# Third block, joint stretch: the head norms' root and reciprocal as one power on GpSimd, 128x512 at a time

## The reference, cut to what matters

```
def rms_norm(x, g):
    xf = x.astype(jnp.float32)
    y = xf * lax.rsqrt(jnp.mean(jnp.square(xf), axis=-1, keepdims=True) + RMS_EPS)
    return y * g

def l2_normalize(x):
    xf = x.astype(jnp.float32)
    return xf * lax.rsqrt(jnp.sum(jnp.square(xf), axis=-1, keepdims=True) + RMS_EPS)

# gdn_mixer: after the short convolution and silu
    q = l2_normalize(q.reshape(B, T, GDN_HEADS, GDN_HEAD_DIM))
    k = l2_normalize(k.reshape(B, T, GDN_HEADS, GDN_HEAD_DIM))
# third_block: the attention's output, per head
    o_na = rms_norm(o_na, na_norm_g[l]).reshape(B, T, NA_WIDTH).astype(x.dtype)
```

## Time and profile before

| what | value |
|---|---|
| median of 3 runs | 4870.76 us (4870.22 to 4872.85) |
| profiled execution, its own time | 4873.72 us |
| its span, first to last instruction | 4872.4 us |
| busy over the span: PE, PEld, DVE, ACT, POOL | 85%, 66%, 39%, 28%, 8% |
| mean granted TensorE clock | 0.914 of full speed |

### The profile page before, as it was taken

The page is one execution under the profiler, slowest core; times in us unless marked ns, Lnnn a source line. Parts: engine busy times, 40 slices in busy tenths (PEclk is TensorE's granted clock), DMA queues, the critical chain, the costliest instruction groups (busy, mean ns, idle before and its releaser), DMA issues. The chain is left out here.

```text
span 4872.4 us, 52741 instructions
## 1 busy us (share of the span) xinstructions
PE 4119.7 (85%) x19748; PEld 3208.3 (66%) x19748; DVE 1906.7 (39%) x2890; ACT 1376.7 (28%) x2125; POOL 394.7 (8%) x260
## 2 busy tenths in 40 slices
PE   5876999996998879999995787885687687999997
PEld 2653478774767758888884565554576565888885
DVE  2135232214465443222234255653544455332333
ACT  3224221212465141111112355562221222111111
POOL 0010000000004100000003000002223211000002
PEclk7987999997999989999997798997898888999999
DMA  1101011111112111111110211111101000111111
GB/s 58 39 13 43 0 52 48 43 40 57 42 34 79 35 48 48 48 47 47 52 41 8 75 37 37 45 48 69 36 1 35 18 27 27 48 47 48 51 48 52
DMA packets 77748, 203.59 MB, mean 42 GB/s; under 512 B 18176, under 2 KB 19520, under 8 KB 77448
## 3 DMA queue, kind: packets, MB, share of 16 engines
q1 hardware_dynamic: 77576, 201.35, 12.8%
HBM read 188.14 MB, written 15.14 MB: 42 GB/s over the span
## 5 line engine op out<-in xcount | busy, mean ns | idle before, releaser
L462 PE MATMUL b_ffn_acc<-b2f_x_lo,b_ffn_wh 128*128 128x512 f32 x832 | 327.5, 394 | 0.0
L461 PE MATMUL b_ffn_acc<-b2f_x_hi,b_ffn_wh 128*128 128x512 f32 x832 | 325.5, 391 | 0.7 <-DVE b_ffn_wl L521 0.7
L463 PE MATMUL b_ffn_acc<-b2f_x_hi,b_ffn_wl 128*128 128x512 f32 x832 | 325.4, 391 | 0.0
L477 ACT ACTIVATE b_ffn_wh<-b_ffn_raw 128x1024 fp32r<-128x1024 f32 (+2 forms) x148 | 149.3, 1009 | 615.7 <-PE b_ffn_acc L463 612.1
L521 DVE TENSOR_TENSOR b_ffn_wl<-b_ffn_raw,b_ffn_wh 128x1024 fp32r<-128x1024 f32 (+2 forms) x148 | 184.9, 1250 | 234.0 <-ACT b_ffn_wh L477 202.9
L461 PE MATMUL b_ffn_acc<-b3f_x_hi,b_ffn_wh 128*128 128x512 f32 x512 | 201.3, 393 | 18.0 <-DVE b_ffn_wl L521 18.0
L462 PE MATMUL b_ffn_acc<-b3f_x_lo,b_ffn_wh 128*128 128x512 f32 x512 | 203.2, 397 | 0.0
L463 PE MATMUL b_ffn_acc<-b3f_x_hi,b_ffn_wl 128*128 128x512 f32 x512 | 200.1, 391 | 0.0
L461 PE MATMUL b_ffn_acc<-b3f_hidden_hi,b_ffn_wh 128*128 128x512 f32 x512 | 199.2, 389 | 0.0
L463 PE MATMUL b_ffn_acc<-b3f_hidden_hi,b_ffn_wl 128*128 128x512 f32 x512 | 199.2, 389 | 0.0
L462 PE MATMUL b_ffn_acc<-b3f_hidden_lo,b_ffn_wh 128*128 128x512 f32 x512 | 199.2, 389 | 0.0
(11 more groups left out here) (549 smaller groups left out, 9242.9 us busy)
## 6 DMA issues: line engine op xcount, KB each, us to landing
b_ffn_raw<-w SPq DMA_DIRECT2D x64, 512.0 KB, 3.3
b_ffn_raw<-w_ffn SPq DMA_DIRECT2D x44, 512.0 KB, 3.5
b_out_raw<-w_out SPq DMA_DIRECT2D x16, 512.0 KB, 3.4
b_ffn_raw<-w_ffo SPq DMA_DIRECT2D x16, 512.0 KB, 3.4
g_heads<-na_done SPq DMA_DIRECT2D x16, 512.0 KB, 2.9
na_feed_raw<-w_gqkv SPq DMA_DIRECT2D x24, 256.0 KB, 2.9
all_x<-xT SPq DMA_DIRECT2D x8, 512.0 KB, 6.6
b_v_raw<-w_bv SPq DMA_DIRECT2D x16, 256.0 KB, 2.6
```

Source lines behind the costliest of these rows:

```text
L461: nc.tensor.matmul(acc[i][:, c], wh[i][:, wk], xh[:, c], start=(k == 0), stop=False)
L462: nc.tensor.matmul(acc[i][:, c], wh[i][:, wk], xl[:, c], start=False, stop=False)
L463: last = nc.tensor.matmul(acc[i][:, c], wl[i][:, wk], xh[:, c], start=False, stop=(k == st.KT - 1))
L477: nc.scalar.activation(wh[i][:, 0:st.KT * P], raw[i][:, 0:st.KT * P], ACT.Copy).then_inc(hi_done, 1)
```

## The change

The copy out of the accumulation bank adds 1e-6 on the way (Identity with a bias in place of Copy). The square root on ACT and the two reciprocals on DVE go. GpSimd gets a strand of its own: after its memsets it fills a 128x1 column with -0.5 and raises each half of `na_norm_root` to that power, once the half's copy is there. The scalings on DVE are as before, at the same due times, and wait for `inverted`, which GpSimd now increments.

```diff
@@ HeadNorms.__init__
+        self.power = ph.sb(f"{name}_power", [P, 1])
-        self.copied, self.rooted = ph.sem(f"{name}_copied"), ph.sem(f"{name}_rooted")
+        self.copied = ph.sem(f"{name}_copied")
@@ HeadNorms.roots
-                self.nc.scalar.activation(self.root[:, c], self.bank[:], ACT.Copy).then_inc(self.copied, 1)
-            yield self.starts[m] + 6.0
-            se.wait_ge(self.copied, 2 * m + 2)
-            self.nc.scalar.activation(self.root[:], self.root[:], ACT.Sqrt, bias=1e-6).then_inc(self.rooted, 1)
+                self.nc.scalar.activation(self.root[:, c], self.bank[:], ACT.Identity, bias=1e-6).then_inc(self.copied, 1)
+
+    def powers(self, pool):
+        self.nc.gpsimd.memset(self.power[:], -0.5)
+        pool.drain()
+        for m in range(len(self.jobs)):
+            for half in range(2):
+                c = slice(half * HALF, (half + 1) * HALF)
+                pool.wait_ge(self.copied, 2 * m + half + 1)
+                self.nc.gpsimd.tensor_tensor(self.root[:, c], self.root[:, c], self.power[:].broadcast_to([P, HALF]), ALU.pow).then_inc(self.inverted, 1)
@@ HeadNorms.scaling
-            for half in range(2):
-                c = slice(half * HALF, (half + 1) * HALF)
-                yield self.starts[m] + 7.5 + 0.7 * half
-                if half == 0:
-                    ve.wait_ge(self.rooted, m + 1)
-                self.nc.vector.reciprocal(self.root[:, c], self.root[:, c]).then_inc(self.inverted, 1)
@@ neighbourhood_attention, block.gpsimd
                 pool.drain().then_inc(padded, 1)
+                norms.powers(pool)
```

## The result

The changed kernel takes 6655.49 us (6648.05 to 6656.54) against 4871.81 us before in the same runs: a ratio of 1.3656, 95% interval 1.3632 to 1.3680, 1783.7 us more. The forecast was 5004 us, its range ended at 5290. The sign was right; the size was not, by a factor of 13.

What follows compares the result with a forecast made beforehand. No engine was full; waits between in-order engines, with norm jobs in DVE's queue, set the stretch. Delay 118 plus port 33 less ACT's 18 gave +133 us, so 5004 us; forecast range 4910 to 5150, whole range 4800 to 5290.

Steps and rivals of the forecast that it cites:

- What comes, and its price: On POOL, 24 powers of 128x512, each taken as two reciprocal-like steps of 6.1 us: 12.3 us.
- the upper end: Longest time allowed for one POOL power: four reciprocal-like steps, 24.5 us.
- First copy's end + 2t: Earliest start of DVE's second scaling, after two successive POOL powers of t each: 24.6 us at t = 12.3.
- 24t - 162: Kernel's time change in us, t being one power's duration: +133 at 12.3 us, break-even at 6.75.
- The windows: From a norm job's first copy's end to DVE's second scaling: twelve before the change, sum 176.9 us, mean 14.7.
- +33: Cost in us of DVE's taps, low parts and other window work pushed aside by POOL's powers.
- -18: Credit in us for work ACT sheds, about half of 35.8 us.
- The rival (c): Power far dearer than two hard steps, POOL becoming the stretch's bound: +426 us, 5297 us at t = 24.5; chance 0.12.
- The port: DVE's two-input instructions and POOL's contend for SBUF ports, locked for a whole instruction; 33 us added.
- ACT's relief: ACT sheds roots, their table loads and six loads back, 35.8 us in all; 18 credited.
- The rival (a): Cheap power on POOL, the change pays: -66 us at t = 4, at most 115 us gained; chance 0.24.

Runs made afterwards that it cites:

- the single power: Kernel before, only the first half of the eleventh norm job through GpSimd's power: 4941.9 us, ratio 1.0140; with its scaling planned late, 4864.72 us, ratio 0.9985.
- the plain multiplications above: Kernel before, plus 300 plain 128x512 multiplications on GpSimd scratch tiles from the joint stretch's start, results unused: 4931.48 against 4870.86 us, ratio 1.0125.
- that run: Changed kernel with the power replaced by a multiplication by 0.001 on GpSimd, norms not computed: 4805.17 against 4875.99 us, ratio 0.9855.

## Why the prediction was wrong

**The step that failed** is "What comes, and its price". It took 12.3 us for a power, from two steps each as hard as DVE's reciprocal at POOL's plain rate, and closed the range at four such steps, 24.5 us. It measured 81.9 us, 6.7 times the 12.3 and thirteen of the steps of 6.1. The 6.1 us that the value and the upper end came from was itself built, from DVE's reciprocal and the ratio of two plain instructions, and no row shows how POOL computes a power. "At least" two such steps is also the wording of a floor, not of a ceiling. So the upper end was not a bound, and it carried the 5290. What takes POOL 0.159 us per column inside a power no run shows.

**The mechanism and its multiplier were right.** "First copy's end + 2t" is what the timeline shows (163.9 us), and with t = 81.9 the sum 24t - 162 gives +1804 us; measured is +1784, within 1.2%. The windows alone give +1789, so the agreement says nothing for the terms +33 and -18, which all but cancel. With powers as long as these the multiplier also no longer tests DVE's order, since 24t of GpSimd's own time fills the stretch; that the order matters is shown by the single power. The rival (c), power far dearer, POOL the stretch's bound, is the case that came, at a size beyond its own number. It had a chance of 0.12.

**The port** was far cheaper than +33. Nine powers beside the stretch cost nothing. In the changed kernel DVE's busy time fell by 60 us though 79.7 us of reciprocals went, so the rest of its work took 19 us longer. Of these, 11 us are the scalings (26.8 us in place of 15.7), and after one that begins beside the job's second power DVE soon waits for that power anyway. The trace of before showed the port for additions, and the plain multiplications above show it again, 61 us for 300 of them. But it doesn't carry over to a power, which holds DVE for 0.8 of its 81.9 us. That it has then read its operands, and works on without them, would explain this, but no run shows it. The Trainium skill's rule (SBUF — State Buffer, "Who interferes with whom"), that the pair is held for the whole instruction, agrees with the addition (3.19 us in place of 1.23 beside 2.40) and not with the power.

**ACT's relief** came as counted: 37 table loads are left in the stretch of 55 (18 + 12 + 7), 18 fewer. That half of it, the 18 us of the sum, would count in time no run shows. Identity with a bias needed none and took 0.60 us, as taken.

**At the cheap end** the sum was a line drawn too far: at 1.04 us it says -137 us, measured was -71. In that run the twelve windows still add up to 89 us, 3.0 to 12.3 each, where 2t would make 25: with a cheap operation something else in DVE's order comes last. The rival (a) named 66 us at t = 4 and a cap of 115; this order gave 71 at t = 1.04.

## What to carry to other kernels

When the one unknown of a change is the duration of an operation that no row shows, a figure built from other operations is no bound from above; here the bound was short by a factor of 3.3 and the value by 6.7. What could be known was the multiplier, 24 us of kernel per us of instruction, and with such a multiplier the operation is measured by itself first. A slow instruction on an idle engine costs if some busy engine's fixed order has its result early: one power of 82 us cost 69 us in place and nothing with its scaling 76 planned us later. It costs in any order once all of them together outlast the stretch, as 1966 us did in 532. And where a price goes by columns, data that is replicated over the partitions should be computed once, compactly, and spread afterwards.

## What the runs showed of the hardware that I had not expected

- A float32 power on GpSimd takes 0.159 us per column plus some 0.4: 81.9 us for 128x512, 41.1 for 128x256, 64x256 and 16x256 alike, 1.64 for 128x8. A multiplication of 128x512 takes 1.04.
- It makes no difference to it whether the exponent is -0.5, 0.5, 1 or 2 (41.1 to 41.2 us for 128x256).
- Beside a running power DVE's two-input instructions keep their time (0.74 us), but for one that meets its first 0.8 us (1.53 in place of 0.69); beside plain multiplications back to back the median of the taps rises from 0.75 to 1.06, with the same longest time of 1.53.
- ACT changed tables between Ln and Exp each time, though both were asked for back to back: 24 loads for 12 pairs.
